# One ScalarE copy for the transposed softmax weights of two heads, over two neighbouring PSUM banks

## What is computed

```python
def causal_block_attention(q, k, v, scale):          # layer 0: 8 heads ("mla")
    ...
        s = jnp.einsum('bqhd,bkhd->bhqk', qb, k, preferred_element_type=jnp.float32) * scale
        p = masked_softmax(s, key_pos[None, :] <= q_pos[:, None])
        return jnp.einsum('bhqk,bkhd->bqhd', p.astype(v.dtype), v)

# layer 1 ("nsa"), one block of queries: 16 heads, each with selected blocks and with a window
        p_s = masked_softmax(s_s, (kpos <= t[None, None, :, None])[:, :, None])
        o_s = jnp.einsum('bghqm,bgqmd->bqghd', p_s.astype(dt), v_sel)
        ...
        p_w = masked_softmax(s_w, m_w)
        o_w = jnp.einsum('bghqk,bkgd->bqghd', p_w.astype(dt), v_wb)
        return gb[..., 0:1] * o_c + gb[..., 1:2] * o_s + gb[..., 2:3] * o_w
```

## Time and profile before

| | us |
|---|---|
| median of 3 runs | 1658.51 |
| lowest, highest | 1657.92, 1660.65 |
| run of the profiled execution | 1665.82 |
| span of the profiled execution | 1664.0 |

### The profile page before, as it was taken

How to read it: one execution, slowest core, us unless ns; L and a number is a source line. 1 busy time by engine, 2 the same in 40 slices (tenths; PEclk the granted TensorE clock), 3 DMA queues, 4 the chain that set the end, 5 groups by cost and what they waited for, 6 DMA issues and landing times.

```text
span 1664.0 us, 25498 instructions
## 1 busy us (share of the span) xinstructions
PE 1638.2 (98%) x9631; PEld 1398.4 (84%) x9631; DVE 1148.8 (69%) x1626; ACT 916.7 (55%) x1470; POOL 116.4 (7%) x130
## 2 busy tenths in 40 slices
PE   8999999999999999999999999999999999999999
PEld 6888897788888888898688888987888889788887
DVE  6766655666667666678966666886867678777776
ACT  6444565554445444535854444675655567655554
POOL 0000011000001000042000000040000003110000
PEclk9999998999999999999999999999999999999999
DMA  8555451465554555442045555443455545245552
GB/s 279 197 192 182 150 199 51 150 238 194 178 200 167 188 185 193 160 145 102 27 173 194 180 198 178 152 111 119 177 195 179 193 165 153 102 152 181 179 198 98
DMA packets 42669, 276.76 MB, mean 166 GB/s; under 512 B 7121, under 2 KB 8034, under 8 KB 9826
## 3 DMA queue, kind: packets, MB, share of 16 engines
q1 hardware_dynamic: 40882, 271.00, 46.7%
q0 software_dynamic: 1712, 4.73, 1.3%
HBM read 274.66 MB, written 1.05 MB: 166 GB/s over the span
## 4 chain that ended last, share of the span: by engine, by line
PE 93%; DVE 3%; ACT 3%; issue 1%; DMA 0%; POOL 0%; SPq 0%; ACTq 0%; DVEq 0%; POOLq 0%
PE bank L786 29%; PE bank L804 22%; PE bank L787 15%; PE bank L730 3%; PE bank L689 2%; PE bank L690 2%; PE bank L691 2%; PE bank L937 2%; PE bank L938 2%; PE bank L939 2%; PE bank L972 1%; PE bank L989 1%; PE bank L1009 1%; PE bank L1053 1%; PE bank L852 1%; ACT xt_both L1441 1%
## 5 line engine op out<-in xcount | busy, mean ns | idle before, releaser
L786 PE MATMUL bank<-xt_both,w_hi 128*128 128x512 f32 x2112 | 746.9, 398 | 2.9 <-DVE xt_both L1931 2.2
L1894 DVE TENSOR_TENSOR w_lo<-raw,w_hi 128x2048 fp32r<-128x2048 f32 (+1 forms) x254 | 580.3, 2286 | 172.7 <-ACT w_hi L1412 170.9
L787 PE MATMUL bank<-xt_both,w_lo 128*128 128x256 f32 x2112 | 590.1, 279 | 0.0
L1412 ACT ACTIVATE w_hi<-raw 128x2048 fp32r<-128x2048 f32 (+1 forms) x254 | 484.9, 1910 | 62.9 <-PE bank L691 41.8
L786 PEld LDWEIGHTS bank<-xt_both,w_hi 128*128 128x128 f32 x2112 | 397.2, 188 | 102.5 <-issue 3.7
L787 PEld LDWEIGHTS bank<-xt_both,w_lo 128*128 128x128 f32 x2112 | 398.6, 189 | 2.3
L1636 ACT ACTIVATE KT<-bank 128x256 f32<-128x256 f32 x264 | 86.9, 381 | 337.2 <-PE bank L787 337.1
L804 PE MATMUL bank<-w_hi,h_lo 128*128 128x512 f32 x528 | 208.3, 394 | 0.0
L804 PE MATMUL bank<-w_lo,h_hi 128*128 128x512 f32 x528 | 208.2, 394 | 0.0
L804 PE MATMUL bank<-w_hi,h_hi 128*128 128x512 f32 x528 | 208.2, 394 | 0.0
L804 PEld LDWEIGHTS bank<-w_hi,h_hi 128*128 128x128 f32 x528 | 99.5, 188 | 23.3 <-issue 0.2
(11 more groups left out here) (345 smaller groups left out, 2039.4 us busy)
## 6 DMA issues: line engine op xcount, KB each, us to landing
raw<-in_stream SPq DMA_DIRECT2D x254, 1024.0 KB, 4.9
work<-in_rpb POOLq DMA_DIRECT2D x32, 64.0 KB, 6.6
X<-in_x SPq DMA_DIRECT2D x2, 512.0 KB, 5.5
raw<-in_stream SPq DMA_DIRECT2D x2, 512.0 KB, 6.6
prob<-in_cmp_w POOLq DMA_DIRECT2D x1, 1024.0 KB, 7.1
O<-in_cmp_w POOLq DMA_DIRECT2D x1, 1024.0 KB, 12.3
out<-X SPq DMA_DIRECT2D x4, 256.0 KB, 2.1
cst<-in_consts SPq DMA_DIRECT2D x1, 712.0 KB, 10.0
```

The source lines that it names most:

```text
L786: pe.matmul(both, w_hi[:, sl, cols], xt_both[:, :, k, :], start=(k == 0), stop=False)
L787: ins = pe.matmul(dst[:, 0:S], w_lo[:, sl, cols], xt_hi[:, k, :], start=False, stop=(k == KD - 1))
L1412: act.activation(to, src, ACT.Copy).then_inc(hi_done, 1)
L1894: dve.tensor_tensor(to, src, hi.bitcast(F32), ALU.subtract).then_inc(lo_done, 1)
```

## The change

The eight PSUM tensors of one bank each become one tensor over all banks, and `bank[i]` becomes its i-th piece, at the same place. ScalarE's `evac` copies both jobs of a duo with one instruction, whose pattern is 2 runs of 384 columns, 512 apart, on both sides: banks 2 and 3 in PSUM, the two halves of `KT` in SBUF. It waits for `t_done` of both jobs and for `pv_done` of both jobs of the duo before, and counts `pt_evac` up by two. Nothing else changes on any engine.

```diff
-        bank = [ctx.enter_context(nc.psum_tensor(f"bank{i}", [P, 512], F32)) for i in range(8)]
+        psum = ctx.enter_context(nc.psum_tensor("bank", [P, 8 * 512], F32))
+        bank = [psum[:, i * 512:(i + 1) * 512] for i in range(8)]
...
-                def evac(i):
-
-                    act.wait_ge(t_done, j0 + i + 1)
-                    if i >= 2:
-                        act.wait_ge(pv_done, j0 + i - 1)
+                def evac(m):
+
+                    i = 2 * m
+                    act.wait_ge(t_done, j0 + i + 2)
+                    if m:
+                        act.wait_ge(pv_done, j0 + i)
                     n = P * len(pt_blocks(jobs[i]))
-                    act.activation(pts_of(i, 0, n), bank[T_BANKS[i % 2]][:, 0:n], ACT.Copy).then_inc(pt_evac, 1)
+                    at = T_BANKS[0]
+                    src = psum[:, at * 512:(at + 2) * 512].rearrange("p (h s) -> p h s", h=2)[:, :, 0:n]
+                    dst = KT[:, 0:1024].rearrange("p (h s) -> p h s", h=2)[:, :, 0:n]
+                    act.activation(dst, src, ACT.Copy).then_inc(pt_evac, 2)
...
                     if 1 <= m <= n_duos(stage):
-                        evac(2 * m - 2)
-                        evac(2 * m - 1)
+                        evac(m - 1)
```

## The result

| | before | changed |
|---|---|---|
| first timing, median of 9 runs, us | 1658.92 | 1662.31 |
| second timing (its before: 33 runs), median of 11, us | 1658.62 | 1661.65 |
| third timing (its before: 21 runs), median of 11, us | 1659.80 | 1659.76 |
| span of the profiled execution, us | 1664.0 | 1660.8 |

The ratio changed to before is 1.0025 (95% interval 1.0017 to 1.0033) in the first timing, 1.0015 (1.0005 to 1.0024) in the second and 1.0006 (0.9997 to 1.0015) in the third. The forecast was +0.6 us and at most 1661.8. The measured median of 1662.31 lies above that range. One run of the kernel before, of 1774.1 us, was in a slow state and is left out of every comparison.

What follows compares the result with a forecast made beforehand. TensorE was taken to bound the kernel, with ScalarE mattering only where TensorE waits for it. +0.06 us in the steady part and +0.5 us at two waits gave +0.6 us, 1658.5 to 1659.1 us; range 1657.2 to 1661.8.

Steps and rivals of the forecast that it cites:

- What bounds the kernel: Whole kernel: TensorE, busy for 98% of the span; a ScalarE saving counts only where TensorE waits for ScalarE.
- The start of the copy: Steady part of nsa: the copy would start 0.09 + 0.01 us after the end of values.
- I take 0.01 us: Extra delay of the copy for the later of two pv_done, taken from bounds of nothing and 0.1 us.
- The length: One copy of 768 columns would take 0.81 us, against 0.87 us for the pair; upper bound 0.98 us.
- The steady part: Duos 2 to 13 of nsa: 0.03 us lost and gained by turns, about 0, put at +0.06 us for rounding.
- what is late next is the copy: In every other steady duo of nsa, turn_p would wait for the copy, at 1.05 us, instead of the exponentials.
- the 0.06 us wait: TensorE's wait for the exponentials before scores in every other steady duo of nsa, 6 times, expected to go.
- the two places: mla's turn_p(2) and nsa's turn_p(14), with no scores left to issue: +0.25 and +0.20 us, +0.5 together with longer first matmuls.
- Where it costs nothing: Duo 0 of nsa and mla, mla's duo 2, nsa's last two duos: later copies are covered by other work, no loss.
- `mla`'s duo 0, with its bound of 0.3 us: First duo of mla, same form as nsa's: put at nothing, with 0.3 us as the most it could cost.
- The signs of being wrong: Copy of 0.9 us or more, steady part faster by over 0.3 us, or the 0.5 us loss absorbed further on.
- The range: Median of the changed kernel: 1657.2 to 1661.8 us, taking in -0.35 and +2.8 us and the spread of a median.

Runs made afterwards that it cites:

- the last run: Changed kernel with one count and one signal a duo, and two copies as before at mla duo 1 and nsa duo 13: 1659.09 us, ratio 0.9998.

## Why the prediction was wrong

*What bounds the kernel.* Right. The copy's saving on ScalarE bought nothing, and a longer copy went straight onto TensorE's path.

*The start of the copy.* Here the step "I take 0.01 us" for the second `pv_done` failed. The records bear out that the two matmuls end 7 ns apart. But what the copy waits for is the signal, and the second signal lands 43 ns after the first. The copy started 0.154 us after `values`, not 0.10. The runs divide the excess: 22 ns for the count by two, which I had not priced at all though the diff shows it; 25 ns for waiting for the second of two signals in place of a lone one; some 10 ns in the landing of a lone signal, which stay open. The 43 ns stand in the trace of the kernel before and could have been read there. My own upper bound for this step, 0.1 us, would have held it, and I didn't carry it into the sum or the range.

*The length.* Right: 811 ns for 0.81 us. The row of a repeated pattern told the price of a pattern over two banks.

*The steady part.* The mechanism was right, "what is late next is the copy", and the 0.06 us wait went. The term was mis-sized, +0.06 us for +1.1 (six times 5.946 - 5.763 us). Of each 0.18 us for two duos, 0.11 is the later start. 0.06 is a piece that I named for the two places and left out here: a `turn_p` that has to wait takes 0.85 us in place of 0.82. Before it TensorE was ready at 1.02 or 1.08 us and the copy was forecast for 1.05, so there was no room for another 0.05 us, and twelve repeats make it the largest term. Mending the signals gives back only the later start: in the last run two duos still take 5.85 us, 0.09 more than before.

*The two places.* The mechanism was right and nothing took up the loss. +0.25 and +0.20, rounded to 0.5 together, were 0.33 and 0.28: the same 0.05 us at the start and 0.03 on the first matmul.

*Where it costs nothing.* Right for `nsa`: with the two places put back, what is left of its loss, 51.74 - 50.73 = 1.0 us, is the steady part's. `mla`'s duo 0, with its bound of 0.3 us, stays untested: every trace with two copies in that duo has a stretch at half clock while `mla` runs. That the stages' 1.7 us agree with the time at equal clock leaves about 0.3 us for it.

*The signs of being wrong.* None of the three that I named came: the copy takes 0.81 us, the steady part does not speed up, and nothing absorbs the loss at the two places. I had named no sign for a slower steady part; only the period, 5.95 us against 5.76 within 0.02, shows it.

*The section that the prediction took from the Perfetto Trace Analysis page of the Trainium skill*, that breaking up the instructions of an engine that isn't saturated but causes bubbles on others may let work be completed sooner, held at both places: the pair put back there won 0.6 us of stage length. What it says of grouping, that it can improve throughput where the engine is saturated, found no case here: ScalarE was busy for 31.53 of 34.8 us before and TensorE for 34.65, and grouping won no time in any run.

*The range.* With +1.75 us for +0.6 at equal clock, the centre should have been 1660.3. Most of the rest of the miss, by the estimate above 1.4 of 2.0 us, is the clock: I read the spread of three runs, 2.7 us, as that of the measurement, while runs of one kernel range from a clock of 0.991 to 1.000, and the three medians of the changed kernel lie between 1659.76 and 1662.31. That the first lies above 1661.8 and the third inside the range is chance, most of it the clock's; the loss in `nsa` is the same in all three traces. The chance of 0.06 for slower by over 0.2% was too low for a loss of 0.11% measured with such a scatter.

## What to carry to other kernels

Merging the two copies saved what their overlap had left, 0.06 us here, and a merged instruction turns "the first half is ready" into "all is ready" for whoever waits. Look for that waiter before counting the saving, and, in a loop where the waiting engine has no room, price each wait to the hundredth and multiply by the repeats. In this kernel a merged copy did best when it counted by one and waited for one signal. Before two kernels are compared within 0.3%, compare the granted clock of their runs.

## What the runs showed of the hardware

- An instruction on ScalarE that counts a semaphore up by two starts 22 ns later after its wait than one that counts by one (0.154 and 0.132 us, 0.112 and 0.091 us). Its waits stand in an instruction of the sequencer that takes 38 ns; with a count by one, 17 ns.
- Two matmuls that end 7 ns apart and count up one semaphore have their signals 43 ns apart (0.008 and 0.050 us after the end of `values`). A copy that waits for the second starts 25 ns later than one that waits for a lone signal of the same matmul (0.132 and 0.107 us).
- A copy over two PSUM banks in runs of 384 or 512 columns costs what its columns cost: 811 ns for 768, 1025 ns for 1024.
- Stretches of 3.4, 6.8 or 13.7 us at half clock (granted 0.51 to 0.54 in the rows) come and go between runs of one kernel, some of them with TensorE busy throughout.
